# Twenty-two expert units kept ahead, the last quad's result returned turned, and weight splits ahead of the convolution's taps

## What is computed

```python
gate = (jax.nn.one_hot(g_sel, N_GROUPS)[:, :, None] * local_w[:, None, :] * g_w[:, :, None]).reshape(S, N_EXPERTS)
a = jnp.einsum('sd,edf->sef', hr, w_gate)          # hr: the normed rows, 1024 wide
u = jnp.einsum('sd,edf->sef', hr, w_up)            # 32 experts, f = 256
act = jax.nn.silu(a) * u * gate[:, :, None]
x = x + jnp.einsum('sef,efd->sd', act, w_down)
...
h = rmsnorm(x, g_mix)
z = h @ w_in                                       # 7 groups of 1024 columns
rnn_x, rnn_y, conv_b, conv_c, conv_x, gate_rnn, gate_conv = jnp.split(z, IN_OFFSETS, axis=-1)
rnn_x = causal_depthwise_conv(rnn_x, conv4_w) + conv4_b
y_rnn = jax.nn.gelu(rnn_y) * rg_lru(rnn_x, w_rg_r, b_rg_r, w_rg_i, b_rg_i, lru_lambda)
y_conv = conv_b * causal_depthwise_conv(conv_c * conv_x, conv3_w)
```

## Time and profile before

| | |
|---|---|
| time, median of 3 runs (lowest to highest) | 854.52 us (853.46 to 856.09) |
| the profiled execution: time, span | 852.39 us, 850.6 us |
| mean granted TensorE clock | 0.982 |
| TensorE matmuls busy | 802.4 us (94%) |
| VectorE busy | 493.6 us (58%) |
| ScalarE busy | 416.1 us (49%) |
| bytes moved by DMA | 214.47 MB, 252 GB/s over the span |

### The profile page before, as it was taken

The page is one execution under the profiler, slowest core; times in us unless marked ns, Lnnn a source line. Parts: engine busy times, 40 slices in busy tenths (PEclk is TensorE's granted clock), DMA queues, the critical chain, the costliest instruction groups (busy, mean ns, idle before and its releaser), DMA issues.

```text
span 850.6 us, 13779 instructions
## 1 busy us (share of the span) xinstructions
PE 802.4 (94%) x5546; PEld 656.0 (77%) x5546; DVE 493.6 (58%) x832; ACT 416.1 (49%) x708; POOL 20.1 (2%) x41
## 2 busy tenths in 40 slices
PE   9999999999999976788879999999999999999996
PEld 7888888888965543444349899999988888888886
DVE  6667777865542110110047899898976555555486
ACT  5777488666411100100246757575746344444466
POOL 1700000000000000000000000000000000000000
PEclk9999999999999988989999999999999999999999
DMA  9855533977899999999984847465574665655521
GB/s 323 270 192 186 174 112 99 342 300 297 302 384 424 423 425 422 425 423 424 417 284 154 268 127 245 149 221 168 203 253 155 221 188 196 197 170 185 188 99 50
DMA packets 95184, 214.47 MB, mean 252 GB/s; under 512 B 4728, under 2 KB 59552, under 8 KB 81824
## 3 DMA queue, kind: packets, MB, share of 16 engines
q1 hardware_dynamic: 93456, 211.70, 68.3%
q0 software_dynamic: 1376, 1.89, 0.8%
q10 hardware_dynamic: 304, 0.20, 0.1%
HBM read 212.72 MB, written 1.05 MB: 251 GB/s over the span
## 4 chain that ended last, share of the span: by engine, by line
PE 62%; DVE 12%; SPq 11%; DMA 7%; issue 4%; ACT 3%; DVEq 1%; ACTq 0%
PE bank L2212 13%; PE bank L2214 13%; PE bank L2213 13%; SPq L829 11%; DMA embed<-in_expert_w_down_dram 4%; PE bank L2229 4%; PE bank L2225 3%; PE bank L2722 3%; DVE w_lo L455 2%; DVE w_lo L453 2%; PE bank L2219 2%; PE bank L2220 2%; DMA stage<-in_w_in_dram 2%; PE bank L2759 2%; DMA whole<-in_expert_w_down_dram 1%
## 5 line engine op out<-in xcount | busy, mean ns | idle before, releaser
L2212 PE MATMUL bank<-w_hi,xT_hi 128*128 128x512 f32 (+2 forms) x390 | 150.9, 387 | 0.0
L2214 PE MATMUL bank<-w_hi,xT_lo 128*128 128x512 f32 (+2 forms) x390 | 148.5, 381 | 0.0
L2213 PE MATMUL bank<-w_lo,xT_hi 128*128 128x512 f32 (+2 forms) x390 | 148.2, 380 | 0.0
L2954 PE MATMUL bank<-hT_hi,w_hi 128*128 128x256 f32 x440 | 122.2, 278 | 1.7 <-DVE w_lo L455 1.0
L2955 PE MATMUL bank<-hT_lo,w_hi 128*128 128x256 f32 x440 | 121.5, 276 | 0.0
L2956 PE MATMUL bank<-hT_hi,w_lo 128*128 128x256 f32 x440 | 121.5, 276 | 0.0
L453 DVE TENSOR_TENSOR w_lo<-stage,w_hi 128x1024 fp32r<-128x1024 f32 (+3 forms) x78 | 87.8, 1126 | 29.5 <-ACT w_hi L439 28.5
L439 ACT ACTIVATE w_hi<-stage 128x1024 fp32r<-128x1024 f32 (+3 forms) x80 | 78.6, 983 | 26.9 <-PE bank L2214 13.3
L455 DVE TENSOR_TENSOR w_lo<-stage,w_hi 128x1024 fp32r<-128x1024 f32 (+3 forms) x78 | 87.6, 1123 | 0.0
L2954 PEld LDWEIGHTS bank<-hT_hi,w_hi 128*128 128x128 f32 x440 | 82.6, 188 | 2.9 <-DVE w_lo L455 2.1
L2214 PEld LDWEIGHTS bank<-w_hi,xT_lo 128*128 128x128 f32 x390 | 73.3, 188 | 14.2
(11 more groups left out here) (485 smaller groups left out, 1603.2 us busy)
## 6 DMA issues: line engine op xcount, KB each, us to landing
stage<-in_w_in_dram SPq DMA_DIRECT2D x36, 1024.0 KB, 5.4
stage<-in_w_gate_up_dram SPq DMA_DIRECT2D x44, 512.0 KB, 4.7
whole<-in_expert_w_up_dram SPq DMA_DIRECT2D x11, 1024.0 KB, 26.0
stage<-in_w_down_dram SPq DMA_DIRECT2D x11, 1024.0 KB, 4.8
whole<-in_expert_w_gate_dram SPq DMA_DIRECT2D x9, 1024.0 KB, 24.9
stage<-in_w_out_dram SPq DMA_DIRECT2D x8, 1024.0 KB, 5.3
stage<-in_cross_w_kv_dram SPq DMA_DIRECT2D x7, 1024.0 KB, 8.7
whole<-in_expert_w_down_dram SPq DMA_DIRECT2D x6, 1024.0 KB, 23.4
```

The source lines that it names most:

```text
L2212: mm(o, k_hi, v_hi, start=start, stop=False)
L2213: mm(o, k_hi, v_lo, start=False, stop=False)
L2214: return mm(o, k_lo, v_hi, start=False, stop=stop)
L2954: mm(o, w_hi[:, s, at:at + P], hT_hi[:, k, :], start=k == 0, stop=False)
```

## The change

1. Memory. `route` becomes a view of `xg`; `xg`, `slot_of` and `token_gates` move into the experts' own memory, and what `xg`, `slot_of` and an unused tensor took is one more place, `turned_unit`. `places` has 20 entries in another order, so 22 units are kept ahead. `weigh()` goes before `gather_scaled(0)`, since both use the shared memory.
2. The last quad. The sums over quads 0 to 6 are copied to `x` and transposed into banks 0 to 3 (`turn_sums`) between `columns(7, 0)` and `columns(7, 1)`. The products of the last quad are then added twice: in transposed form onto these banks (`add_turned`, the rounded and remaining parts as weights) for the projection, and in row form in banks 6 and 7 (`rows_back`), from where VectorE adds them to `x` (`add_rows`). `down` is called for each half of the columns apart, and `bring_back` ends with quad 6. The `mix` transposes go, and so does the tensor `zeros`.
3. The overflow branch stands ahead of quad 7 on each engine (on SP ahead of the first loads of the heads).
4. In a head, VectorE's splits of RG_I and G_R move up, to before the product of the convolution's inputs and to behind its first tap.

```diff
-    places = [spent_unit[:], over_latent[0], over_latent[1], over_turned, over_queries, whole_of(embed), over_scores,
-              stage[:, 2], stage[:, 0], stage[:, 1], over_values, whole_of(x), HI[2], LO[2], HI[0], LO[0], HI[1], LO[1], whole_of(raw_turned)]
+    places = [spent_unit[:], whole_of(embed), stage[:, 2], stage[:, 0], stage[:, 1], over_latent[0], over_scores, over_latent[1],
+              over_turned, over_queries, over_values, whole_of(raw_turned), HI[1], LO[1], HI[2], LO[2], HI[0], LO[0], whole_of(x), turned_unit[:]]
...
-        for u, units in ((U_CO + 1, (14, 15)), (U_CO + 2, (16, 17)), (U_CO + 3, (ROWS_UNIT, 18, 19))):
+        for u, units in ((U_CO + 1, (16, 17)), (U_CO + 2, (18, 19)), (U_CO + 3, (ROWS_UNIT, 14, 15, 21))):
...
-        load_expert(sp, 20)
+        load_expert(sp, 13)
         sp.wait_ge(sem("norm_sums"), nth(NORMS, "moe"))
         sp.wait_ge(sem("x_kept"), 4)
-        load_expert(sp, 13)
+        load_expert(sp, 20)
...
+        weigh()
+        dve.wait_ge(sem("token_gates"), 2)
         gather_scaled(0)
-        weigh()
         count_overflow()
... ScalarE
+        copy_sum(0)
+        copy_sum(1)
+        expert_quad(QUADS - 1)
...
+        def mix_high(n):
+            act.wait_ge(sem("mix_turned"), n + 1)
+            for j in range(2):
+                k = 2 * n + j
+                ins = nc.scalar.activation(hT_hi[:, k], bank[n][:, 256 * j:256 * j + 256], ACT.Copy, scale=gain_of(MIX_G, k))
+            ins.then_inc(sem("xT_hi"), 1)
...
+        down_high(QUADS - 1, 0)
+        mix_high(0)
+        mix_high(1)
+        for t in range(T):
+            mix_squares(0, t)
+        down_high(QUADS - 1, 1)
+        first_columns_hi(0)
+        mix_high(2)
+        mix_high(3)
         first_columns_hi(1)
         split_hi(act, SLOT, U_HEADS + 1)
-        mix_squares(0, 0)
-        mix_squares(0, 1)
         mix_squares(1, 0)
         mix_squares(1, 1).then_inc(sem("norm_sums"), 1)
... VectorE
+        down_low(QUADS - 1, 0)
+        mix_low(0)
+        mix_low(1)
+        add_rows(0)
+        down_low(QUADS - 1, 1)
+        first_columns_lo(0)
+        mix_low(2)
+        mix_low(3)
         first_columns_lo(1)
+        add_rows(1)
         split_lo(dve, SLOT, U_HEADS + 1)
...
             link(stt(y_in[:], y_tanh[:], 1.0, y_in[:], ALU.add, ALU.mult))
+            unit(RG_I)
             dve.wait_ge(sem("c_copied"), h + 1)
...
             for f in range(2):
                 ins = ts(conv3[:, f], cpad[:, f, 0:256], col(conv3_w, 0, f), None, ALU.mult)
+            unit(G_R)
             for tap in range(1, 3):
...
-            unit(RG_I)
-            unit(G_R)
             unit(G_C)
... TensorE
+        def turn_sums():
+            pe.wait_ge(sem("sums_copied"), 4)
+            view = x[:].rearrange("p t (k q) -> p t k q", k=KD)
+            for n in range(4):
+                for j in range(2):
+                    for t in range(T):
+                        mm(bank[n][:, 256 * j + P * t:256 * j + P * t + P], view[:, t, 2 * n + j], ident, start=j == 0 and t == 0, stop=False, is_transpose=True)
+        def add_turned(c, y, low):
+            for n in (2 * c, 2 * c + 1):
+                for j in range(2):
+                    at = 256 * n + P * j - 512 * c
+                    ins = mm(bank[n][:, 256 * j:256 * j + 256], y[:, c, at:at + P], token_now[:].rearrange("p t s -> p (t s)"), start=False, stop=low and j == 1)
+                if low:
+                    ins.then_inc(sem("mix_turned"), 1)
+        def rows_back(c, y, low):
+            for t in range(T):
+                ins = mm(bank[6 + t][:, :], token_now[:, t], y[:, c], start=not low, stop=low)
+                if low:
+                    ins.then_inc(sem("rows_returned"), 1)
...
+        down(last, 0)
+        pe.wait_ge(sem("token_now"), QUADS)
+        pe.wait_ge(sem("expert_y_hi"), 2 * last + 1)
+        add_turned(0, y_hi, False)
+        rows_back(0, y_hi, False)
+        pe.wait_ge(sem("expert_y_lo"), 2 * last + 1)
+        add_turned(0, y_lo, True)
+        rows_back(0, y_lo, True)
+        down(last, 1)
+        pe.wait_ge(sem("expert_y_hi"), 2 * last + 2)
+        add_turned(1, y_hi, False)
+        pe.wait_ge(sem("expert_y_lo"), 2 * last + 2)
+        add_turned(1, y_lo, True)
+        def last_rows():
+            pe.wait_ge(sem("x_moe"), 2)
+            rows_back(1, y_hi, False)
+            rows_back(1, y_lo, True)
```

More of the change, by code:

```diff
@@ L125, in program @@
     x = sb("x", [P, T, D])
-    zeros, ones, before_it = (sb(n, [P, P], F32R) for n in ("zeros", "ones", "before_it"))
+    ones, before_it = (sb(n, [P, P], F32R) for n in ("ones", "before_it"))
     xs = sb("xs", [P, T, D])
@@ L880, in _ @@
         sp.wait_ge(lo_ready, U_CO + 3)
-        load_expert(sp, 10)
+        load_expert(sp, 4)
         been_read(sp, "pT")
@@ L911, in _ @@
         over_flag = overflow(sp)
-        sp.wait_ge(sem("gates_done"), QUAD * QUADS)
-        for j in range(RING):
-            load_head(0, j)
         with sp.If(over_flag > 0):
@@ L2745, in turn_hidden, with down, downs_here @@
             ins.then_inc(sem("expert_turned"), 1)
-        def down(q):
+        def down(q, c):
             units = [QUAD_UNITS * q + QUAD * 2 + j for j in range(QUAD)]
+            if q == QUADS - 1 and c:
+                pe.wait_ge(sem("last_halves"), 16 * QUAD)
+            for k in range(2):
+                at = D * k + 512 * c
+                for j, i in enumerate(units):
+                    ins = mm(bank[4 + c][strip(j), :], hiddenT[:, k, strip(j)], expert_unit(i)[:, at:at + 512], start=k == 0, stop=k == 1)
+                    if k == 1:
+                        ins.then_inc(sem("downs_done"), 1)
+        def downs_here(q):
             units_here(pe, q, 2)
@@ L2752, in down @@
             pe.wait_ge(sem("rows_ready"), 2 * min(q + 2, QUADS))
-            for c in range(2):
-                if q == QUADS - 1 and c:
-                    pe.wait_ge(sem("last_halves"), 16 * QUAD)
-                for k in range(2):
-                    at = D * k + 512 * c
-                    for j, i in enumerate(units):
-                        ins = mm(bank[4 + c][strip(j), :], hiddenT[:, k, strip(j)], expert_unit(i)[:, at:at + 512], start=k == 0, stop=k == 1)
-                        if k == 1:
-                            ins.then_inc(sem("downs_done"), 1)
         def bring_back(q):
@@ L2793, in embed_products, with quad @@
                 ins.then_inc(sem("embed_filled"), 1)
-        gather(0)
-        for q in range(QUADS):
+        def quad(q):
             columns(q, 0)
             turn_slots(q)
+            if q == QUADS - 1:
+                turn_sums()
             columns(q, 1)
@@ L2802, in _ @@
             turn_hidden(q)
-            if q == QUADS - 1:
-                pe.wait_ge(sem("embed_copied"), 4)
+            downs_here(q)
+        gather(0)
+        for q in range(QUADS - 1):
+            if q == QUADS - 2:
                 over_flag = overflow(pe)
-            down(q)
+            quad(q)
+            for c in range(2):
+                down(q, c)
             bring_back(q)
```

200 lines of the change are left out of this document (102 added, 98 removed), and 1 row of the table products.

## The result

The changed kernel takes 859.39 us (median of 6 runs, 858.18 to 859.80), the kernel before 854.62 in the same comparison (6 runs, 853.46 to 856.09): ratio 1.0062, interval 1.0049 to 1.0074. It is slower, by 4.8 us; I had forecast 851.7 and given "slower" 0.07. The profiled execution took 858.64 (span 856.8, before 850.6).

A forecast was written before the change was run, and what follows sets the result against it. Expert weight transfers bound the kernel from about 230 to 435 us, then TensorE's start and the heads. Terms -1.5 + 0.35 + 0.8 - 2.5 = -2.85 us gave 849.5 profiled, 851.7 median; range 849.5 to 854.0.

The forecast's parts named there:

- slower: Whole kernel: slower by more than 0.3% (2.56 us), chance 0.07.
- E: Ahead of the last quad: the jump over the overflow block delays the experts' end; at 4 us, 855.7; chance 0.06.
- Transfers, -1.5: Experts' weight loads: unit 21 fills the dry queue before the first reload at 243.36; -1.5 us, bounds -2.5 and 0.
- Rival B: Experts' transfers end no earlier, the raggedness after 243 belonging to the reloads; -1.35 us, 853.2; chance 0.12.
- `weigh` at nothing: Ahead of the gather: `weigh()` fits into VectorE's idle time and costs nothing; uncovered it would be 1.8 us.
- Last quad, +0.35: Last quad's return: saved transposes and copies paid back by squares ahead of ScalarE's second high copy; +0.35 us.
- Clock, +0.8: After the last quad: TensorE's idling drops its clock to 1.2 GHz for 3.4 us; +0.8 us, bounds 0 and 1.7.
- Splits ahead of taps, -2.5: In the heads: earlier RG_I and G_R splits end TensorE's waits for low parts; -2.5 us, bounds -0.5 and -2.7.
- rival D: Heads don't gain: VectorE waits before G_R's split, making taps, scan and next splits late; -0.55 us, 854.0; chance 0.08.

The follow-up runs named there:

- e2: The kernel before with 64 bytes more ahead of `hT_hi`, nothing else changed: 858.14 us, ratio 1.0057 to the kernel before.
- e6: The changed kernel with 192 bytes ahead of the recurrent layer's tensors: 850.38 us, ratio 0.9967 to the kernel before.
- e4: The changed kernel with the splits of RG_I and G_R back in their old places: 859.81 us, ratio 1.0078 to the kernel before.
- e5: The changed kernel with 88 short series of products behind its end, to measure their pace at different places of weights and rows; its whole time says nothing.
- e11: e6 with 24 series of 42 products behind its last product, TensorE waiting for ScalarE after each; whole time says nothing, heads 166.7 us.
- e13: The changed kernel with 448 bytes ahead of the recurrent layer's tensors: 851.80 us, ratio 0.9974 to the kernel before.
- e10: e6 with 19 places and 21 units kept ahead, `turned_unit` unused: 852.93 us, ratio 0.9994 to the kernel before.
- e7: e6 with the first half's squares moved behind the second high copy and high parts in ScalarE's queue: 853.71 us, ratio 0.9990 to the kernel before.
- e8: e7 with VectorE's split of G_R moved ahead of the second convolution's first products: 852.28 us, ratio 0.9984 to the kernel before.
- e14: e13 with the first half's squares moved back in ScalarE's queue as in e7: 854.18 us, ratio 0.9985 to the kernel before.
- e9: e6 with the splits of RG_I and G_R in their old order: 854.55 us, ratio 1.0016 to the kernel before.

## Why the prediction was wrong

The step that failed is one that I didn't count as a step: "4 products of 256 columns at 0.114 us, from 41.22/363", and after it "TensorE is busy throughout the heads then; nothing more comes out of this". TensorE's price of a product was carried over from the earlier trace rows as if it belonged to the shape. It belonged to the shape and to the place: the change moved `hT` from a distance of 448 bytes to 256. The table shows that to be 5 to 6 ns a product; 64 bytes, to a distance of 0, cost the kernel before 0.57% in e2; and going back to 448 took 9.2 us out of the changed kernel's heads (170.0 to 160.8 in e6). The sum lacked a term of +9.6 us, which would have made it +6.8. Measured is +4.8 in the medians and +6.2 between the two profiled executions (852.39 and 858.64), whose paces are known. The changed kernel had 120 in each profile of its place (e4's and e5's too), while the runs of before reach from 850.97 to 857.39, as if some of them had the second pace. That would bring the medians closer; it is shown for e6's kernel (e11), not for before. No rival had the term; E, the one on the slower side, was about the jump, and no refill shows at the last quad's columns (TensorE 0.8 us earlier there than before).

With the place put right, the forecast sum, -2.85 us, meets e6's -2.7 (853.05 to 850.38) and e13's -2.3. That is partly luck, since two errors cancel: in e6's profile the second columns start 2.1 us later than before (448.03 for 445.95; forecast 0.35 earlier, as -1.5 + 0.35 + 0.8), and the heads are 4.3 us shorter (160.8 for 165.1; forecast 2.5). The terms:

- *Transfers, -1.5.* The mechanism was right: unit 21 issued at 230.62, the reload still at 243.09, share 0.98 in place of 0.87. The size was too large: some 0.8 by the start of the last quad's downs (430.33 for 431.21; 0.5 in e6 against e10). The windows show where the rest went: 399 GB/s for 315 in 243 to 251, but 420 for 423 in 251 to 425, which is 1.2 us of transfer. All 15 profiled executions of the changed kernel and its variants have 419 or 420 there, e10 with its 21 units ahead among them, and e2, with the old places, has 423 as before. So the lower rate goes with the change, not with the 22nd unit; that it is the new order of places was not tested. Rival B is out: in e10 the dip came back with the dry queue.
- *`weigh` at nothing.* Right: the reloads didn't move.
- *Last quad, +0.35.* The order was right to the instruction. TensorE's idling was 2.50 us where I had 437.8 to 440.55, and e7 shows the price of the squares' place, 1.7 us of idling. The three terms ahead of the heads together were forecast at -0.35; the second columns start at 446.39 for 445.95, so +0.4, most of the difference being the transfers.
- *Clock, +0.8.* It fell where I said in the changed kernel, and the work that bounds felt it for some 2 us (starts 0.21 apart up to 443.4). What brings the fall isn't shown. e7 and e8, with idling of 0.8 us, have 1.00 in 440 to 444; but e14, with the same 0.80 us, has 0.57 there, as the changed kernel has. And in e6 and e7 the clock was low earlier, ahead of this idling (0.66 and 0.72 in 430 to 436). No run changed the idling alone.
- *Splits ahead of taps, -2.5.* With the place put right the mechanism holds and the size was too small: e6's heads have no wait and are 4.3 us shorter than before, where I had summed 2.5 us of idling. A wait costs more than the idling shown for it: the one of 1.52 us at 474.16 is 1.80 us from start to start, where 0.11 is the pace. e9 against e6 gives 4.2 in the medians, of which the waits are 1.0 us; its profiled execution also has the second pace. In the changed kernel as it was measured the term is worth nothing, since at a pace of 120 TensorE doesn't wait with the old order either (e4).

The second lesson is in e7 and e8: the 2 us that I had named as lost to ScalarE's queue can be won ahead of the heads, but no median shows the gain. In their profiled executions TensorE reached a split too early by 0.1 and 0.5 us, and the second pace behind it cost more than was won. This looks like rival D's kind of wait, at a price which the table of waits doesn't show. Whether the waits bring that pace is open, as e11, e13 and e14 have it without any.

## What to carry to other kernels

When a change moves tensors, the instructions that read them may get another price though nothing in the code of that stage changed: compare starts of a long run of equal products, in ns, before looking at waits, and keep the distance between TensorE's weights and rows modulo 512 bytes when memory is dealt out anew. A mean in a page's group that moves from 276 to 283 over 1440 instructions is 10 us. A stretch of TensorE without waits is worth more than the sum of the idling: 4.3 us for 2.5 here. And one profiled execution isn't enough where a program has two paces: e6's kernel showed one in three profiles and the other in a fourth.

## What the runs showed of the hardware

- Products of 128 x 256 in fp32r come every 113.3, 118 or 120 ns at 2.4 GHz (272, 283 and 288 cycles), by how far the rows start behind the weights: with weights at 128 modulo 512, 113.3 (114 in the short series of e5) at distances 192 and 448, 118 to 118.5 at 64, 128, 320 and 384, 119 to 120 at 0 and 256. The Trainium skill (TensorE: Matmul & The Clock Gate, Back-to-back issue gap) gives 262 cycles for 256 columns as the gap of isolated products; the best in this kernel, with new weights for each product, is 272. The Trainium skill (SBUF — State Buffer, SBUF: two separate sides) says that of the engines' reads only the port shared by GpSimd and VectorE contends; the table, taken with those engines quiet, shows 6% by the distance between two operands of TensorE.
- Products of 128 x 512 have their best distances where those of 256 have their worst. By how far the rows start behind the weights they come every 227 to 228 ns at 0 and 256, every 229 to 230 at 64 and 320, and every 232 to 234 at the other four.
- In the fast place there is a second pace, 117.8. In series behind the kernel's end it came behind transposes or a wide product (24 of 24 series), not behind a wait that ScalarE ended, and in 4 of 12 series behind a wait that VectorE ended. In the kernels the same transposes are followed by either pace, also in two executions of the same code (e6 and e11). The pace then stays up to the next break, over 1176 products in e7.
- The expert transfers ran at 423 GB/s in 251 to 425 in both profiled executions with the old places and at 419 or 420 in all 15 of the changed kernel and its variants.
